# The delta rule's state kept in two forms, and the attention's keys and updates issued inside its chunk steps

## The reference

```python
def step(s, inp):                       # rwkv7_recurrence, one frame
    sa = einsum('bhvk,bhk->bhv', s, kk_t)
    s = s * w_t - sa[..., None] * (kk_t * a_t) + v_t[..., None] * k_t
    return s, einsum('bhvk,bhk->bhv', s, r_t)
...
b = jnp.cumsum(gc, axis=2)              # GLA, one chunk of 64 frames
o = einsum('bhld,bhdv->bhlv', qc * exp(b), s) + (within the chunk)
s = s * exp(b_last)[..., None] + einsum('bhld,bhlv->bhdv', kc * exp(b_last - b), vc)
```

## Time and profile before

| | us |
|---|---|
| median of 3 runs | 1468.71 (1468.45 to 1468.92) |
| profiled execution, its own time | 1471.95 |
| span of the profiled execution | 1470.2 |
| PE busy | 1426.2 (97%) |
| DVE busy | 1172.7 (80%) |
| ACT busy | 950.9 (65%) |

### The profile page before, as it was taken

One profiled execution on the slowest core, in us unless ns is written; L12 is line 12 of the kernel. 1 busy time (PEld: TensorE's weight loads), 2 busy tenths in 40 slices (PEclk: granted clock), 3 DMA queues, 4 the chain that ended last, 5 costly groups with the idle time before them and its releaser, 6 DMA issues.

```text
span 1470.2 us, 29344 instructions
## 1 busy us (share of the span) xinstructions
PE 1426.2 (97%) x11325; PEld 1275.4 (87%) x11326; DVE 1172.7 (80%) x1580; ACT 950.9 (65%) x1257; POOL 76.5 (5%) x152
## 2 busy tenths in 40 slices
PE   7999989999999999999999999999999999999997
PEld 7988978999999899888788888888888888888884
DVE  5686578555535789867998998899989899898997
ACT  4464455433333796476677887778777887877873
POOL 8400000000000000000000000000000000000000
PEclk9999999999999999999999999999999999999999
DMA  8531004544445362217999999999999999999992
GB/s 262 157 100 35 2 17 145 171 144 148 157 133 165 91 182 88 87 59 284 324 391 396 402 391 398 349 396 384 369 398 346 410 379 363 398 350 410 392 344 93
DMA packets 162214, 371.62 MB, mean 253 GB/s; under 512 B 10232, under 2 KB 85968, under 8 KB 162128
## 3 DMA queue, kind: packets, MB, share of 16 engines
q1 hardware_dynamic: 159352, 361.18, 67.1%
q0 software_dynamic: 2160, 7.87, 2.0%
q10 hardware_dynamic: 616, 1.37, 0.2%
HBM read 360.68 MB, written 9.71 MB: 252 GB/s over the span
## 4 chain that ended last, share of the span: by engine, by line
PE 87%; DVE 7%; ACT 3%; issue 1%; DMA 1%; SPq 0%; DVEq 0%; ACTq 0%
PE psum L1367 11%; PE psum L1368 11%; PE psum L1369 11%; PE psum L595 10%; PE psum L596 9%; PE psum L597 9%; PE psum L1391 5%; PE psum L1393 5%; PE psum L1392 5%; PE psum L711 2%; PE psum L1376 1%; PE psum L1129 1%; DVE wd_lo L1464 1%; PE psum L695 1%; DVE w_lo L2180 1%
## 5 line engine op out<-in xcount | busy, mean ns | idle before, releaser
L2180 DVE TENSOR_TENSOR w_lo<-moe_ring,w_hi 128x1024 fp32r<-128x1024 f32 (+1 forms) x560 | 608.4, 1155 | 30.3 <-ACT w_hi L2912 30.3
L2912 ACT ACTIVATE w_hi<-moe_ring 128x1024 fp32r<-128x1024 f32 (+1 forms) x560 | 532.1, 1014 | 72.0 <-PE psum L1393 39.0
L1367 PE MATMUL psum<-w_hi,xe_hi 128*128 128x512 f32 (+1 forms) x768 | 288.8, 376 | 3.1 <-DVE xe_lo L2361 1.8
L1368 PE MATMUL psum<-w_hi,xe_lo 128*128 128x512 f32 (+1 forms) x768 | 286.4, 373 | 0.0
L1369 PE MATMUL psum<-w_lo,xe_hi 128*128 128x512 f32 (+1 forms) x768 | 286.0, 372 | 0.0
L1464 DVE TENSOR_TENSOR wd_lo<-arena,wd_hi 128x1024 fp32r<-128x1024 f32 x141 | 169.9, 1209 | 132.9 <-ACT wd_hi L2437 132.5
L595 PE MATMUL psum<-in_hi,wd_hi 128*128 128x320 f32 x800 | 250.5, 313 | 1.8 <-DVE wd_lo L1464 1.2
L2437 ACT ACTIVATE wd_hi<-arena 128x1024 fp32r<-128x1024 f32 (+1 forms) x140 | 146.1, 1047 | 157.0 <-PE psum L597 151.9
L597 PE MATMUL psum<-in_hi,wd_lo 128*128 128x320 f32 x800 | 247.2, 309 | 0.0
L596 PE MATMUL psum<-in_lo,wd_hi 128*128 128x320 f32 x800 | 247.2, 309 | 0.0
L1367 PEld LDWEIGHTS psum<-w_hi,xe_hi 128*128 128x128 f32 x768 | 144.9, 189 | 30.0 <-DVE w_lo L2180 2.5
(11 more groups left out here) (449 smaller groups left out, 1791.0 us busy)
## 6 DMA issues: line engine op xcount, KB each, us to landing
moe_ring<-in_moe_w SPq DMA_DIRECT2D x216, 1024.0 KB, 8.8
moe_ring<-in_moe_w SPq DMA_DIRECT2D x64, 768.0 KB, 5.2
arena<-in_ffn_w SPq DMA_DIRECT2D x30, 1024.0 KB, 5.3
arena<-in_w_in_c SPq DMA_DIRECT2D x16, 1024.0 KB, 5.5
arena<-in_w_in_ab SPq DMA_DIRECT2D x12, 1024.0 KB, 5.3
arena<-in_w_out_ab SPq DMA_DIRECT2D x4, 1024.0 KB, 5.1
arena<-in_w_out_c SPq DMA_DIRECT2D x4, 1024.0 KB, 5.0
arena<-in_ffn_w SPq DMA_DIRECT2D x4, 768.0 KB, 4.4
```

Source lines behind the costliest of these rows:

```text
L1367: pe.matmul(b[:, 0:w], xe_hi[:, k, :], hi_[:, c0:c1], start=(k == 0), stop=False)
L1368: pe.matmul(b[:, 0:w], xe_lo[:, k, :], hi_[:, c0:c1], start=False, stop=False)
L2180: dve.tensor_tensor(w_lo[:, i % UNITS, 0:unit_words(i)], moe_unit(i), w_hi[:, i % UNITS, 0:unit_words(i)], ALU.subtract)\
L2912: act.activation(w_hi[:, i % UNITS, 0:unit_words(i)], moe_unit(i), ACT.Copy).then_inc(S("e_hi"), 1)
```

## The change

The carried state of the prompt is kept in two forms. `Hnew` is the state after a chunk, not yet decayed; PE uses it for the next chunk, and the decay that it lacks has been multiplied into that chunk's inputs beforehand: `PRC` of chunks 1, 2 and 3 by `dC` of the chunk before, one DVE operation each (128x8x64), in levels 2, 3 and 4 of the loop. `H[:, 0]` is the decayed state, which DVE makes after `h_done` and counts in a new semaphore `h_kept`; the next state is `H[:, 0] + dh`, written to `Hnew`. In step 0, `Hnew` is a plain copy of dh, with `h_done` behind it, ahead of the add and the multiply for the sample's state.

`chain_operands` moves from step 1 to step 0 on DVE, `norm_totals` from the end of step 2 to a place behind step 2's `W1s` copy. On PE the keys of chunks 0 to 3 move to step 1 and those of chunk 4 to step 2, both into bank 0, and the GLA's updates move from behind step 3 into step 3, into banks 2, 3 and 0 instead of 1, 2 and 3; `turn` is advanced by three so that all later banks stay what they were. ACT copies the keys in steps 1 and 2.

```diff
+        Hnew = m2.take(CW).rearrange("p (f n) -> p f n", f=RF)
...
-            def gla_keys(two):
+            def gla_keys(j, k):
                 pe.wait_ge(*at_count("gla_qk", 1))
-                for j, chunks in enumerate(GLA_CHUNKS):
-                    b = take(("gla_tk", j), "gla_tm", 4 + j, two[j])
+                b = take(("gla_tk", j), "gla_tm", 4 + j, k)
...
-            def gla_updates():
+            def gla_updates(at_):
                 pe.wait_ge(*at_count("gla_tm", 5))
                 for g, chunks in enumerate(GROUPS):
-                    b = take(("gla_ds", g), "gla_s", (2, 4, 5)[g])
+                    b = take(("gla_ds", g), "gla_s", (2, 4, 5)[g], at_[g])
...
             def carried(c, f):
-                return None if c == 0 else H[:, 0 if c < N_PROMPT_CH else 1, f, :]
+                return None if c == 0 else Hnew[:, f, :] if c < N_PROMPT_CH else H[:, 1, f, :]
...
                 else:
-                    gla_keys(w1_at)
+                    gla_updates([*w1_at, score_at])
+                if 0 < i < 3:
+                    gla_keys(i - 1, score_at)
                 pe.wait_ge(*at_count("u_done", i + 1))
...
-            gla_updates()
+            turn[0] += 3
             pe.wait_ge(*at_count("gn_done", 1))
...
-            pe.wait_ge(*at_count("h_done", len(STEPS)))
+            pe.wait_ge(*at_count("h_kept", len(STEPS)))
...
                 gla_step(lv + 1)
+                if 0 < lv - 1 < N_PROMPT_CH:
+                    c = lv - 1
+                    dve.tensor_tensor(PRC[:, :, :, chunk(c)], PRC[:, :, :, chunk(c)],
+                                      dC[:, :, c - 1:c].unsqueeze(2).to_broadcast([P, RF, 2, C]), ALU.mult)
...
                 if i == 0:
                     gla_select(LEVELS)
-                elif i == 1:
                     chain_operands(gla)
+                elif i == 2:
+                    dve.wait_ge(*at_count("o_done", 2))
+                    norm_totals(0, NEARLY)
...
                 for j, c in enumerate(step):
-                    h = H[:, 0 if c < N_PROMPT_CH else 1]
                     d = where["dh", i][:, j * CW:(j + 1) * CW].rearrange("p (f n) -> p f n", f=RF)
-                    decay = dC[:, :, c:c + 1].to_broadcast([P, RF, RN])
                     if c == 0:
-                        mul = dve.tensor_tensor(h, d, decay, ALU.mult)
+                        dve.tensor_copy(Hnew, d).then_inc(S("h_done"), 1)
+                    elif c < N_PROMPT_CH:
+                        dve.tensor_tensor(Hnew, H[:, 0], d, ALU.add).then_inc(S("h_done"), 1)
                     else:
-                        link(dve.tensor_tensor(h, h, d, ALU.add))
-                        mul = dve.tensor_tensor(h, h, decay, ALU.mult)
-                mul.then_inc(S("h_done"), 1)
+                        link(dve.tensor_tensor(H[:, 1], H[:, 1], d, ALU.add))
+                        dve.tensor_tensor(H[:, 1], H[:, 1], dC[:, :, c:c + 1].to_broadcast([P, RF, RN]), ALU.mult)
                 dve.wait_ge(*at_count("h_done", i + 1))
-                if i == 2:
-                    dve.wait_ge(*at_count("o_done", 2))
-                    norm_totals(0, NEARLY)
+                dve.tensor_tensor(H[:, 0], Hnew, dC[:, :, i:i + 1].to_broadcast([P, RF, RN]), ALU.mult).then_inc(S("h_kept"), 1)
+                dve.wait_ge(*at_count("h_kept", i + 1))
...
+                if 0 < i < 3:
+                    gla_rows(2 + i, 3 + i)
                 if i == len(STEPS) - 1:
                     norm_squares(0, NEARLY, 0)
-                    gla_rows(3, 5)
                     norm_std(0, NEARLY, 0)
```

More of the change, by code:

```diff
@@ L774, in gla_values @@
                     mm.then_inc(S("gla_tm_full"), 1)
-            def gla_keys(two):
+            def gla_keys(j, k):
                 pe.wait_ge(*at_count("gla_qk", 1))
-                for j, chunks in enumerate(GLA_CHUNKS):
-                    b = take(("gla_tk", j), "gla_tm", 4 + j, two[j])
-                    for i, c in enumerate(chunks):
-                        for f in range(2):
-                            mm = diag(b, (2 * i + f) * C, gla["KD"][:, f, chunk(c)], ident2[:, :], i == 0 and f == 0,
-                                      c == chunks[-1] and f == 1)
-                    mm.then_inc(S("gla_tm_full"), 1)
-            def gla_updates():
+                b = take(("gla_tk", j), "gla_tm", 4 + j, k)
+                for i, c in enumerate(GLA_CHUNKS[j]):
+                    for f in range(2):
+                        mm = diag(b, (2 * i + f) * C, gla["KD"][:, f, chunk(c)], ident2[:, :], i == 0 and f == 0,
+                                  c == GLA_CHUNKS[j][-1] and f == 1)
+                mm.then_inc(S("gla_tm_full"), 1)
+            def gla_updates(at_):
                 pe.wait_ge(*at_count("gla_tm", 5))
                 for g, chunks in enumerate(GROUPS):
-                    b = take(("gla_ds", g), "gla_s", (2, 4, 5)[g])
+                    b = take(("gla_ds", g), "gla_s", (2, 4, 5)[g], at_[g])
                     for i, c in enumerate(chunks):
```

## The result

| | changed | before |
|---|---|---|
| median of 11 runs each, us | 1476.53 (1473.10 to 1479.38) | 1470.52 (1468.45 to 1472.93) |
| profiled execution, its own time | 1477.09 | 1471.95 |
| its span | 1475.4 | 1470.2 |
| mean granted clock | 0.992 | 0.997 |

A forecast was written before the change was run, and what follows sets the result against it. PE was taken as the bound (87% of the chain of waits); 2.4 us from steps and bank wait plus 1.7 from the clock made 4.1, moving the median from 1468.7 to 1472.8 us, with an 8-in-10 range of 1470.7 to 1475.0.

The forecast's parts named there:

- The wait on the bank: PE's first L806 product waits for DVE's last state, bank 0 being shared: 4.5 us idle, L806 starting at 202.86.
- The clock: PE's groups between 202.86 and in_hi run at half clock after the idle time, costing 1.7 us.
- Rival A: At L806 the wait is paid but the clock stays up: 1471.1 us; chance 0.2.
- The fillers' own lengths: Attention work moved into PE's steps 1, 2 and 3 adds 0.94, 0.23 and 0.97 us.
- the saving of step 0 to 1: DVE's W1s copy after step 0 starts at 183.84 instead of 184.13, saving 0.29 us.
- the three new products on `PRC`: On DVE, about 0.7 us each, lying in gaps where DVE waits for PE, so costing nothing.
- the steps' term, "0.48 late": Chunk steps up to the second norm sums: savings 1.4, fillers 2.1, sums at 197.32 instead of 196.84.
- 0.44 for each decay taken off the path: In steps 1 and 2, DVE's decay behind the add lies beside PE's 0.60, saving 0.44 us each.
- The shift: Nothing between 209 us and the end waits for a transfer, so the delay reaches the end unchanged.
- rival C: Wait costs 4.1; later half-clock stretch falls away (1471.2) or a second comes at the 1.54 gap (1474.4); chance 0.1.
- the first half of C: The half-clock stretch at 696 to 699.7, behind the 1.81 gap, falls away: 1471.2 us.
- A shift of 4.1: Whole-kernel forecast: 2.4 us by steps and bank wait plus 1.7 by clock; chance 0.62.

The follow-up runs named there:

- e3: Changed kernel with the GLA's first outputs in banks 1 and 2 and the sample chunk's in 0 and 3; 1472.74 us against 1471.25, ratio 1.0013.
- e4: Changed kernel with 36 transposes that nothing reads ahead of the bank wait, keeping PE busy; 1471.55 us in one run.
- r1: The changed kernel run again, unchanged; 1477.51 us.
- e7: Kernel before with 384 tiny 16-column products written out in a row ahead of step 0; 766 matmuls took 37.93 us.
- e1: Changed kernel with the attention's keys, updates and key copies put back, keeping the two-form state; 1470.54 us against 1471.25, ratio 0.9995.
- e6: e1 without the chunk's own part of o in steps 1 to 3, 16 matmuls fewer per step; 1467.42 us in one run, before 1470.70.
- e5: Kernel before with 12 tiny products (24 matmuls) per step ahead of PE's wait for DVE; 1471.60 us in one run, before 1470.70.
- e9: Kernel before with 384 products of 64 columns written out without a loop ahead of step 0; 768 matmuls took 19.9 us, kernel 1494.84 us.
- e12: Kernel before delayed by 44 unread transposes ahead of step 0; 1473.58 us, before 1471.64.
- e13: Kernel before delayed by 26 unread transposes ahead of step 0; 1475.19 us, before 1471.64.
- e11: e1 with the last H[:, 0] decay moved behind the centring of the last norm sums on DVE; 1469.61 us against 1471.04, ratio 0.9993.
- e2: Kernel before with only the attention's moves (keys, updates, key copies, chain_operands), state kept as before; 1478.04 us in one run.
- e8: Kernel before with 384 tiny 16-column products as a loop of 12 times 32 ahead of step 0; 766 matmuls took 36.49 us.

## Why the prediction was wrong

**The wait on the bank was right.** 4.51 us idle in front of L806, released by DVE's state line, were forecast as 4.5; e3 takes it away and most of the loss with it. With the clock kept up (e4) the wait's own share is 2.0 against 1.9.

**The clock was right** in place and size: 1.5 against 1.7, over at about 206 and not carried into the projection. Rival A (clock stays up) falls. (In r1 it cost 0.3 more: 31.96 - 26.34 = 5.62 from L806 to the first low half, against 5.35.) The granted clock was 0.50 from 200 us on, with PE idle until 202.65, and stayed there for 3.3 us of work. The Trainium skill (TensorE: Matmul & The Clock Gate, "The HAM clock gate") says that the default state is throttled and that activity releases it. This stretch agrees with it; e7 is against the plain reading, with PE shown busy for more than 30 us and the clock at 0.50.

**The fillers' own lengths were right**, 0.93 against 0.94 for the keys; the saving of step 0 to 1 too (0.29 in r1, e1, e3 and e4; none in the profiled changed kernel, which stopped 0.66 for instructions instead of 0.39 there). That the three new products on `PRC` cost nothing showed too (0.69 us each, with 1.23 to 1.46 of waiting for PE left behind them).

**The step that failed is the steps' term, "0.48 late".** It measured 1.8, and 1.2, 1.0 and 0.7 in r1, e3 and e4, which have the same steps. The working followed who waits for whom and took PE to have its next instruction always at hand. In that it was exact: e6, where PE has them, is 1.4 early as the savings add up to, and e4's `W1s` copies stand at 6.60, 10.75 and 14.27 where it had 6.60, 10.78 and 14.25. The term that it lacked is the supply. It booked 0.44 for each decay taken off the path; the steps were already at 128 matmuls per 3.7 us, so that a shorter path became a stop for instructions (e1: 0.0 at the second norm sums). The fillers are instructions above all: e5 shows what 24 more matmuls per step cost where their time is hidden. Rows of before had only a part of it in view: two periods of 3.71 between 183.53 and 190.95 are 29 ns for each of 128 matmuls, where a group in free flow takes 15. But there the dependencies alone give 3.71 as well, and the instruction queue, whose packets come every 3.5 to 4.2 us there, has no row and no part in the prediction. The Trainium skill (Runtime: NRT & Kernel Launch, "Instruction fetch mechanics") says that an engine refills its code in blocks of 16 KiB by a queue of its own, and that this is hidden, since dispatch is slower than the fill. The traces agree on the block (packets of 16 KB, and 128 matmuls with their 128 loads between two stops). They disagree on the hiding: in e9 the engine goes through a block in 1.9 us and gets one per 3.7.

**The shift was not passed on whole.** The prediction held everything behind 209 us to be unchanged. The traces of the changed kernel lose 1.4 us more there, with a second clock drop. This is the second half of rival C (one more stretch at half clock, 1474.4), at another gap than the 1.54 that it named; its reason, that all reaches the place at another moment, e12 and e13 don't bear out. The old stretch at 695 only moved along with its gap (now 1.82 us, at 700), so the first half of C did not come.

**Sum.** Profiled, from the stage's start: 1.8 + 2.0 + 1.5 + 1.4 = 6.7, less 1.5 for an earlier start of this execution, is the 5.2 between the spans. The medians differ by 6.0. The base drifted as well: 1468.71 was the median of three runs of before, 1470.52 that of eleven. A shift of 4.1 would have been 1474.6 on that base, within the range. The other 1.9 is about what the steps (0.7 to 1.3 more than forecast) and the second drop (1.4) add.

## What to carry to other kernels

Count the instructions of a stretch of small matmuls before adding up its waits: if their number times 29 ns (the pace of e9's code without a loop) reaches the stretch's length, shortening the dependencies gives nothing and every product laid into an idle time is paid for, and a look at the rows for idle times released by "issue", and at the instruction queue, tells it. Short stops don't show as such rows (e11); compare an interval with a kernel that has none. Where work moves ahead, follow the output bank that it takes to its next owner: here one bank number turned a wait on the first read into a wait on the last, which cost 2 us, and the idle time that it made cost 1.5 more by the clock. A change that costs at one place and gains at another is to be run in halves (e1 and e2) before it is kept or dropped as one.

## What was not expected of the hardware

- The supply of instructions above: bursts of exactly 128 matmuls, 3.46 to 4.02 us apart, in code without a loop, and a loop of 64 matmuls that runs at 17 ns each with no packet loaded.
- Products of 16 columns ran at 47 to 49 ns each with the granted clock at 0.50 for over 30 us, and PE shown busy for all of it (e7, e8); those of 64 columns round the four quarters kept 1.00, although e9 stood still for up to 1.92 us between bursts.
- A stop of 2.0 us at L1199 was followed by 0.71 over 5 us in the changed kernel; one of 2.2 at the same place in before was followed by 1.00; in e9, one of 1.92 by 0.71, in e2, 1.91 by 1.00. The length of a gap of this size alone does not decide the clock.
- A stop of 2 us released by "issue" can appear or vanish 430 us behind an edit: with 36 or 44 more transposes far ahead (e4, e12) or 36 more small products (e5) it was gone, with 26 (e13), or with 384 products in a row (e7, e9), it was there. That it is a wait for instructions is the reading of "issue" and of 126 matmuls in a row ahead of it in e9; no run tests it at this place.
